# Three slots for raw weights and four for split ones, in place of four and three

## The reference

```python
def first_block(...):
    for i in range(2):
        if i == 0: h = h + conformer_conv(rms_norm(h), ...)    # pw1, depthwise conv of 31 taps, layer norm, silu, pw2
        else:      h = h + diff_attention(rms_norm(h), ...)    # qkv, 8 heads with a relative bias, w_o
        u = rms_norm(h);  h = h + (silu(u @ w_gate) * (u @ w_up)) @ w_down
        h = h + sigmoid(rms_norm(h) @ ple_w_gate) * (p[i] @ ple_w_proj)
def second_block(...):
    proj = rmsnorm(x) @ w_in                                    # av, au, az, bp, bz, cc, ga, gb, gc
    merged = g0 * (ya @ w_a) + g1 * (yb @ w_b) + g2 * (yc @ w_c)
    return rmsnorm(x + merged @ w_out)
```

## Time and profile before

| | |
|---|---|
| median of 3 runs | 1063.29 us (1062.49 to 1063.47) |
| the profiled execution, its own time | 1062.74 us |
| its span, first to last instruction | 1060.7 us |
| PE busy | 1035.3 us, 98% of the span |
| DVE / ACT busy | 673.9 us (64%) / 513.8 us (48%) |
| DMA moved | 191.67 MB, mean 181 GB/s |
| granted TensorE clock, mean | 0.995 of full |

### The profile page before, as it was taken

How to read it: one execution, slowest core, us unless ns; L and a number is a source line. 1 busy time by engine, 2 the same in 40 slices (tenths; PEclk the granted TensorE clock), 3 DMA queues, 4 the chain that set the end, 5 groups by cost and what they waited for, 6 DMA issues and landing times.

```text
span 1060.7 us, 13676 instructions
## 1 busy us (share of the span) xinstructions
PE 1035.3 (98%) x5554; PEld 873.7 (82%) x5554; DVE 673.9 (64%) x955; ACT 513.8 (48%) x607; POOL 68.4 (6%) x50
## 2 busy tenths in 40 slices
PE   8999999999999999999999999999999999999997
PEld 7977788888877788788888887788888888999886
DVE  5996664545467886874554456766554467777554
ACT  6336444434446576654434435654544544444533
POOL 4881000000000000000000000000000000000000
PEclk9999999999999999999999999999999999999999
DMA  8755855555534532555555543556645454554531
GB/s 313 248 174 116 250 219 190 173 193 198 175 143 159 199 119 80 184 206 216 174 193 199 184 175 118 209 179 238 218 172 188 156 198 163 195 187 171 199 119 40
DMA packets 30382, 191.67 MB, mean 181 GB/s; under 512 B 3689, under 2 KB 6249, under 8 KB 8433
## 3 DMA queue, kind: packets, MB, share of 16 engines
q1 hardware_dynamic: 24912, 179.32, 47.1%
q0 software_dynamic: 2096, 7.79, 3.2%
q10 hardware_dynamic: 3312, 3.71, 1.3%
HBM read 187.58 MB, written 3.21 MB: 180 GB/s over the span
## 4 chain that ended last, share of the span: by engine, by line
PE 89%; DVE 6%; ACT 4%; issue 1%; POOL 0%; ACTq 0%; POOLq 0%; DVEq 0%
PE bank L268 28%; PE bank L270 27%; PE bank L269 27%; DVE w_lo L1261 2%; PE bank L312 2%; ACT w_hi L808 2%; PE bank L459 1%; PE bank L377 1%; PE bank L433 1%; DVE x_lo L1316 1%; DVE arena L1306 1%; ACT x_hi L826 0%; PE bank L514 0%; ACT arena L998 0%; PE bank L471 0%
## 5 line engine op out<-in xcount | busy, mean ns | idle before, releaser
L1261 DVE TENSOR_TENSOR w_lo<-raw,w_hi 128x2048 fp32r<-128x2048 f32 x160 | 366.1, 2292 | 218.9 <-ACT w_hi L808 218.5
L808 ACT ACTIVATE w_hi<-raw 128x2048 fp32r<-128x2048 f32 x169 | 322.4, 1910 | 167.3 <-PE bank L270 154.3
L268 PE MATMUL bank<-w_hi,x_hi 128*128 128x512 f32 x800 | 318.9, 399 | 7.2 <-DVE x_lo L1316 4.8
L270 PE MATMUL bank<-w_hi,x_lo 128*128 128x512 f32 x800 | 313.4, 392 | 0.0
L269 PE MATMUL bank<-w_lo,x_hi 128*128 128x512 f32 x800 | 312.7, 391 | 0.0
L268 PEld LDWEIGHTS bank<-w_hi,x_hi 128*128 128x128 f32 x800 | 151.0, 189 | 42.5 <-issue 7.0
L270 PEld LDWEIGHTS bank<-w_hi,x_lo 128*128 128x128 f32 x800 | 150.9, 189 | 32.6
L269 PEld LDWEIGHTS bank<-w_lo,x_hi 128*128 128x128 f32 x800 | 151.2, 189 | 29.5
L268 PE MATMUL bank<-w_hi,z_hi 128*128 128x512 f32 (+1 forms) x368 | 142.9, 388 | 1.1 <-DVE z_lo L1606 0.7
L270 PE MATMUL bank<-w_hi,z_lo 128*128 128x512 f32 (+1 forms) x368 | 141.7, 385 | 0.0
L269 PE MATMUL bank<-w_lo,z_hi 128*128 128x512 f32 (+1 forms) x368 | 141.6, 385 | 0.0
(11 more groups left out here) (213 smaller groups left out, 783.5 us busy)
## 6 DMA issues: line engine op xcount, KB each, us to landing
raw<-in_ws SPq DMA_DIRECT2D x169, 1024.0 KB, 4.8
arena<-u_scr ACTq DMA_DIRECT2D x16, 142.0 KB, 4.8
arena<-in_rows POOLq DMA_DIRECT2D x2, 1024.0 KB, 5.4
toep<-bias_row POOLq DMA_DIRECT2D x1, 1536.0 KB, 33.9
h<-in_x_tok SPq DMA_DIRECT2D x2, 512.0 KB, 5.0
arena<-in_rows POOLq DMA_DIRECT2D x2, 512.0 KB, 6.6
arena<-toep POOLq DMA_DIRECT2D x1, 1024.0 KB, 7.9
out<-arena SPq DMA_DIRECT2D x2, 512.0 KB, 2.9
```

The source lines that it names most:

```text
L268: pe.matmul(dst, s_hi, m_hi, start=first, stop=False)
L270: return pe.matmul(dst, s_lo, m_hi, start=False, stop=last)
L808: act.activation(w_hi[:, g % SPLIT, :], raw[:, g % RAW, :], ACT.Copy).then_inc(hi_done, 1)
L1261: dve.tensor_tensor(w_lo[:, g % SPLIT, :], raw[:, g % RAW, :], w_hi[:, g % SPLIT, :].bitcast(F32), ALU.subtract).then_inc(lo_done, 1)
```

## The change

```diff
-RAW, SPLIT = 4, 3
+RAW, SPLIT = 3, 4
```

## The result

| | before | after |
|---|---|---|
| median | 1063.29 us (1061.85 to 1063.47, 5 runs) | 1072.13 us (1069.58 to 1075.94, 5 runs) |
| the profiled execution, its own time | 1062.74 us | 1075.94 us |
| its span | 1060.7 us | 1073.9 us |
| granted TensorE clock, mean | 0.995 | 0.992 |

The change makes the kernel slower: ratio 1.009, 95% interval 1.0076 to 1.0105. 1074.9 us was forecast, with 1067.2 to 1077.5 as the range. The profiled execution is the slowest of the five; a second profile of the same kernel is among the experiments, and the reasons are read from both.

What follows compares the result with a forecast made beforehand. PE, busy 98% of the span, bounds the kernel, so only its stalls count. 9.3 + 3.7 - 1.4 = 11.6 us on 1062.74 gives 1074.3, plus 0.55 for the median: 1074.9 us; range 1067.2 to about 1077.5.

Steps and rivals of the forecast that it cites:

- start and conv: Start and conv stage: later loads cost 0; piece 12's load beside conv rows up to 1 us, swallowed at pw2.
- seam 1: pw2, 104 to 123 us: PE begins ffn0 at 128.0, not 120.15; 7.9 us, with the clock 9.3.
- clock behind it: After each PE stall over 2.3 us the granted clock falls to 0.50 for 3 us, costing 1.4 us.
- seam 2: wo, 439 to 461 us: an extra low part ahead of `o_split(1)`; 3.7 us, or 3.0 without a clock fall.
- seam 3: End of ple0 and ple1: the low part goes behind `h_factor`, the waits for L1034 and L1153 go; -1.4 us.
- Steady stretches: Between the seams: the shifts of splits and loads cancel, every engine waits where it did; 0.
- Seam 1, order: pw2: one more low part ahead of chunk 0's add delays PE's chunk 1; 2.3 us, inside the 7.9.
- Seam 1, load: pw2: load 14 takes 14.1 us like the load issued then before, landing at 118.2; PE begins ffn0 9.8 later.
- Rival 1: pw2: load 14 shares with toep, takes 8.4 us, isn't late; 1069.3 us, or 1067.2 without clock falls; chance 0.26.

Runs made afterwards that it cites:

- e1: The changed kernel with the load of piece 12, in place of 13, held until the last conv rows have landed; 1073.89 us.
- e11: The changed kernel with splits two pieces ahead at pw2 and wo and piece 12's load held, toep written in one piece; 1066.52 us.
- e10: The changed kernel with toep written in two steps and piece 12's load held, the order at both seams unaltered; 1065.57 us.
- e7: The changed kernel with splits two pieces ahead at pw2 and wo, piece 12's load held and toep written in two steps; 1059.68 us.
- e4: The changed kernel with the toep transfer moved behind all of pw2; 1082.55 us.
- e5: The changed kernel with toep written in two steps, 8 rows and then a DRAM-to-DRAM copy; 1071.11 us.
- e8: The kernel before with toep in two steps and the norm factor ahead of the last low part of ple0 and ple1; 1060.53 us.
- e12: The changed kernel again, unaltered, for a second profile and more executions; 1071.21 us.
- e3: The changed kernel with splits two pieces ahead, not three, at pw2 and wo; 1066.2 us.

## Why the prediction was right

The forecast was 2.8 us above the median, inside the range and of the right sign. Term by term, with both profiles of the change (us that PE falls behind the kernel before):

| step | forecast | first profile | second profile |
|---|---|---|---|
| start and conv | 0, up to 1 swallowed | 3.3, swallowed | 3.0, swallowed |
| seam 1, PE begins ffn0 | 128.0, +7.9 | 129.65, +9.5 | 128.12, +8.0 |
| clock behind it | 1.4 | 2.9 | 1.6 |
| seam 2 | 3.7, or 3.0 without a fall | 3.7 | 3.0 |
| seam 3 and all else, after seam 1 and after seam 2 | -1.4 | -0.8 and -2.2 | -0.8 and -2.3 |
| sum | 11.6 | 13.1 | 9.5 |

The second column of numbers is the balance above; the third is worked out the same way (319.63, 444.63, 472.71 and the span of 1070.2, against 310.06, 435.81, 460.92 and 1060.7). The spans are 13.2 and 9.5 us longer. The sum is closer than its terms: in the first profile seam 1 and the clock behind it were 3.1 us dearer than forecast, and the last row gave back 1.6 us more. That these partly cancel is luck, and so is part of how near the total came: the two profiles lie 1.5 above and 2.1 below the 11.6.

- **Steady stretches: 0.** Right. Neither profile has a stall in a feed-forward stretch that wasn't there.
- **Start and conv: 0.** The step that failed. "A low part later still leaves each of them more than one piece time" was right for the splits, but what is late is not a split: a load that moved 6.2 us later ran into the store of the conv rows, 2.7 to 6.0 us, and PE lost about 3. The time was saved by the other half of the sentence, that seam 1 swallows it; e1 and e11 show that it does, and e10 that it counts once toep is out of the way.
- **Seam 1, order:** 2.3, measured 2.2 (e10 to e7). Stalls of 2.5 near 107.5 and 4.5 near 123 were forecast; they came at 110.8 (2.35), later by the conv stage, and at 125.2 (4.47), later by the load.
- **Seam 1, load:** the size by the row of the same instant was right; load 14 took 12.4 and 11.2 us in place of 14.1, but was issued 3 us later and landed at 119.8 and 118.3 (forecast 118.2). The 9.8 us from landing to PE's begin were 9.8 in both. "The load lands 2.4 us after that" was read from one row. It held to 0.1 us in seven of the nine profiles named at e4, and within 0.8 us in the other two. As a mechanism, waiting for the end, it fails: e4 shows a load at 22.2 us beside toep, landing ahead of its end. Rival 1 had the sharing right and the price wrong: the load that took 8.4 us was issued 0.4 us behind load 13, which landed at 82.06, so only its last 4 us lay beside toep.
- **Seam 2:** right in both forms: with a fall of the clock 3.7, without it the add bounds PE (a wait of 0.51 us for L1387 in the second profile) and it is 3.0.
- **Seam 3:** the waits went as forecast. Of the 1.6 or so beyond them, 1.15 is the fall of the clock at 651 us of the kernel before, which the changed kernel doesn't have: PE stands 15.43 us behind at the x_lo stall there (666.26 to 650.83) and 14.28 after it (694.68 to 680.40). The forecast had kept that fall.
- **Clock:** 1.4 for each stall over 2.3 us was one of two outcomes, not a price: behind stalls of 2.3 to 2.4 us it cost nothing (chunk 1 of pw2 in both profiles) or up to 1.5 (the same place in e5), and behind the stall of 4.5 it cost 2.9.

By kernels, the 9.3 us between the change (1072.1) and the kernel before (1062.8, as run beside e5 to e8; side by side in e12 they were 8.9 apart) divide so, to within some tenths, as the medians come from several chips: 1072.1 to 1065.6 (e10) are the two collisions of transfers that a missing raw slot brings, with their falls of the clock; 1065.6 to 1059.7 (e7) is the order at pw2 and wo; and e7 stands 3.1 under the kernel before, most of it seam 3.

## What to carry to other kernels

A ring of slots sets not only how far ahead work may run but when each transfer starts: with one slot less, every load is issued one piece later, and what must be checked is what else is on the DMA engines at that new time, loads and small stores alike. A helper that ties "how far ahead" to the number of slots moves bulk work in front of short work that the bottleneck waits for; keep the two apart (e3, e7). And where several stalls end in a wait for one absolute time, mending them one at a time shows nothing (e1) or little (e5), mending all of them shows their sum (e7, e10).

## What the runs showed of the hardware

- A write of 1.5 MB from 8 partitions to DRAM took 33.9 to 35.6 us with half of the DMA engines busy (0.48, 49 GB/s). Written as 8 rows (4.1 to 5.6 us) and then copied from DRAM to DRAM, 1.5 MB again, the second step took 12.3 to 13.2 us in four kernels.
- A load of 1 MB beside it took 22.2 us in place of 4.8, with two more loads in flight behind it, while the write was lengthened by under 2 us (e4). Issued 8 to 12 us before the write's end, a load landed 2.46 to 2.49 us behind that end in seven of nine profiles, 2.83 and 3.17 us in the others.
- A store of 147 KB (128 x 288 fp32) took 6.0 us in place of 2.7 beside a load of 1 MB; with the load held back (e1) it took 3.1.
- The same stall of 2.3 to 2.4 us was followed by a clock of 1.00 in some profiles and by 0.50 for about 3 us in others, of one kernel too (wo in the two profiles of the change). The spans of these two profiles differ by 3.7 us: 2.0 of it lies in falls behind seam 1 and at wo, and 1.5 in the begin of ffn0, where toep's end came 0.9 us sooner. What sets a fall off, and how much of the spread of 6 us between executions it makes, was not shown.
